# Order tables of the two-level product passes and the closing tiles of a Hymba decode step

## The reference, cut to what matters

```python
def layer(h, pos, conv_prev, ret_prev, norm_mix, w_in, conv_w, w_out,
          norm_mlp, w_up, w_down, ret_fn):
    hn = rmsnorm(h, norm_mix)
    z = hn @ w_in
    u_in, c_gate, b_gate, q, k, v, g = jnp.split(z, SPLITS, axis=-1)
    conv_y, conv_state = causal_conv3(conv_prev, c_gate * u_in, conv_w)
    y_conv = b_gate * conv_y
    ...
    o, ret_state = ret_fn(q, k, v, ret_prev.astype(q.dtype))
    y_ret = head_rmsnorm(o).reshape(Bsz, T, RET_WIDTH) * jax.nn.silu(g)
    h = h + jnp.concatenate([y_conv, y_ret], axis=-1) @ w_out
    hn2 = rmsnorm(h, norm_mlp)
    h = h + jnp.square(jax.nn.relu(hn2 @ w_up)) @ w_down
    return h, conv_state, ret_state
...
    y_prompt = rmsnorm(hp, norm_final)[:, N_META:]
    y_sample = rmsnorm(hs, norm_final)
```

## Time and profile before

| | us |
|---|---|
| median of 3 runs | 1171.07 (1168.94 to 1172.07) |
| the profiled execution | 1170.56 |
| its span, first to last instruction | 1168.8 |
| TensorE busy | 1145.3 (98%) |
| VectorE busy | 764.9 (65%) |
| GpSimd busy | 551.0 (47%) |
| ScalarE busy | 434.7 (37%) |
| mean granted TensorE clock | 0.996 |

### The profile page before, as it was taken

How to read it: one execution, slowest core, us unless ns; L and a number is a source line. 1 busy time by engine, 2 the same in 40 slices (tenths; PEclk the granted TensorE clock), 3 DMA queues, 4 the chain that set the end, 5 groups by cost and what they waited for, 6 DMA issues and landing times.

```text
span 1168.8 us, 22531 instructions
## 1 busy us (share of the span) xinstructions
PE 1145.3 (98%) x8689; PEld 1119.8 (96%) x8689; DVE 764.9 (65%) x1141; ACT 434.7 (37%) x853; POOL 551.0 (47%) x541
## 2 busy tenths in 40 slices
PE   9999999999999999989999999999999999999996
PEld 7899999999999999989999999999898999999996
DVE  4355446456355676787777776777866677777756
ACT  6423313214124433533333333335434444444413
POOL 0154242253150431044232322323989998888992
PEclk9999999999999999999999999999999999999999
DMA  6431211211201222254435353437854553454213
GB/s 202 132 110 36 79 50 54 74 54 54 74 19 57 80 89 87 74 163 134 166 118 181 109 166 130 138 120 257 277 186 129 177 169 103 146 176 136 89 38 146
DMA packets 154007, 139.79 MB, mean 120 GB/s; under 512 B 6809, under 2 KB 118146, under 8 KB 153916
## 3 DMA queue, kind: packets, MB, share of 16 engines
q1 hardware_dynamic: 148814, 135.50, 36.3%
q10 hardware_dynamic: 5102, 3.05, 0.9%
HBM read 98.07 MB, written 40.47 MB: 119 GB/s over the span
## 4 chain that ended last, share of the span: by engine, by line
PE 46%; POOL 3%; DVE 3%; DMA 1%; issue 1%; ACT 0%; SPq 0%; ACTq 0%; POOLq 0%; DVEq 0%
PE pair L1819 15%; PE pair L1820 15%; PE pair L1821 15%; POOL dn_lo L755 2%; DMA m_raw<-m_dram 1%; DVE m_lo L1440 1%; DVE y_out L1557 1%; PE pair L1870 0%; DVE hid L1585 0%; POOL dn_s L743 0%; DVE hid L1459 0%; POOL dn_s L745 0%; ACT m_hi L1058 0%; POOL dn_s L748 0%; POOL dn_s L746 0%
## 5 line engine op out<-in xcount | busy, mean ns | idle before, releaser
L1819 PE MATMUL pair<-m_hi,dn_hi 128*128 128x258 f32 x896 | 256.5, 286 | 8.3 <-DVE a L1591 2.8
L1819 PE MATMUL pair<-b_hi,up_hi 128*128 128x258 f32 x896 | 255.0, 285 | 3.2 <-DVE hid L1497 2.2
L1820 PE MATMUL pair<-m_lo,dn_hi 128*128 128x258 f32 x896 | 254.3, 284 | 0.0
L1821 PE MATMUL pair<-m_hi,dn_lo 128*128 128x258 f32 x896 | 254.1, 284 | 0.0
L1820 PE MATMUL pair<-b_lo,up_hi 128*128 128x258 f32 x896 | 253.6, 283 | 0.0
L1821 PE MATMUL pair<-b_hi,up_lo 128*128 128x258 f32 x896 | 252.2, 282 | 0.0
L1620 PE MATMUL pair<-x_hi,w_both 128*128 128x344 f32 (+2 forms) x576 | 188.7, 328 | 0.0
L1622 PE MATMUL pair<-x_hi,w_both 128*128 128x344 f32 (+2 forms) x576 | 184.3, 320 | 0.0
L1621 PE MATMUL pair<-x_lo,w_both 128*128 128x344 f32 (+2 forms) x576 | 184.2, 320 | 0.0
L1819 PEld LDWEIGHTS pair<-m_hi,dn_hi 128*128 128x128 f32 x896 | 169.7, 189 | 11.1 <-POOL dn_lo L755 7.9
L1591 DVE TENSOR_TENSOR hid<-pair,hid 128x516 f32<-128x516 f32 (+1 forms) x194 | 124.5, 643 | 78.9 <-PE pair L1821 77.6
(11 more groups left out here) (205 smaller groups left out, 2141.4 us busy)
## 6 DMA issues: line engine op xcount, KB each, us to landing
m_raw<-m_dram SPq DMA_DIRECT2D x56, 516.0 KB, 5.0
m_dram<-hid SPq DMA_DIRECT2D x64, 258.0 KB, 2.3
up_raw<-w_up_dram SPq DMA_DIRECT2D x32, 512.0 KB, 5.0
dn_raw<-w_down_dram SPq DMA_DIRECT2D x128, 128.0 KB, 2.4
w_raw<-w_in_dram SPq DMA_DIRECT2D x28, 512.0 KB, 3.7
m_dram<-hid SPq DMA_DIRECT2D x16, 774.0 KB, 3.8
h_dram<-hid SPq DMA_DIRECT2D x8, 516.0 KB, 3.2
h_in<-h_dram SPq DMA_DIRECT2D x16, 258.0 KB, 4.3
```

The source lines that it names most:

```text
L1819: m_.matmul(to, shs[k], mhs[k], start=STARTS[i] and k == 0, stop=False, skip_group_check=more)
L1820: m_.matmul(to, shs[k], mls[k], start=False, stop=False, skip_group_check=more)
L1821: ins = m_.matmul(to, sls[k], mhs[k], start=False, stop=k == last, skip_group_check=more)
```

## The change

Four tables of places are rewritten, one copy changes engine, and the closing tiles are cut anew.

1. Up stage, units 0 to 2: `SPLITS` and `LOWS` place the weight parts otherwise; the four `mid_sum` of unit 0 stand behind the read of product 1 and 2 of unit 1, not ahead of them; `scaled(1, .)` stands ahead of `up_low`; some `squared` move by one product.
2. Down stage: `mid_step` gives way to `MID_HIGH` and `MID_LOW`, tables of steps, one pair for block 0 and one for the later blocks; `AHEAD` covers all passes from 5 to 31 by a new formula.
3. Block 0: product 0 is copied from PSUM to `a1` by ScalarE, not VectorE (new semaphore `a1_copied`, for which VectorE and TensorE's product 2 wait).
4. End: the column halves of the last block are 260 and 256; the closing tiles are 0 to 3 as before, then 4 (8 rows, made beside the products), and four late tiles of 128 rows. Six of eight transposes of tile 5 and a first part of its sum of squares stand ahead of the last two products. The norms of tiles 0 to 4 are each written as two halves of 512 values with a read of a product between them.

```diff
-FINAL_AT = {(NW, 3): 0, (NW + 1, 0): 1, (NW + 1, 5): 2, (NW + 2, 3): 3}
-NORM_AT = {(NW + 1, 1): 0, (NW + 1, 3): 1, (NW + 2, 1): 2, (NW + 2, 6): 3}
+FINAL_AT = {(NW, 3): 0, (NW, 6): 1, (NW + 1, 3): 2, (NW + 1, 6): 3, (NW + 2, 2): 4}
+NORM_AT = {(NW, 6): (0, 0), (NW + 1, 0): (0, 1), (NW + 1, 2): (1, 0), (NW + 1, 3): (1, 1), (NW + 1, 6): (2, 0), (NW + 2, 0): (2, 1),
+           (NW + 2, 2): (3, 0), (NW + 2, 3): (3, 1), (NW + 2, 5): (4, 0), (NW + 2, 6): (4, 1)}
+EARLY_AT = (NW + 2, 4)
...
-def mid_step(n):
-
-    return {0: {4: 0}, 1: {1: 1, 4: 2}, 2: {1: 3, 4: 4}, 3: {1: 5, 4: 6}}[n]
+MID_HIGH = ({11: 0, 13: 1, 15: 2, 17: 3, 20: 4, 22: 5, 24: 6}, {4: 0, 6: 1, 8: 2, 12: 3, 15: 4, 19: 5, 22: 6})
+MID_LOW = ({12: 0, 15: 1, 17: 2, 19: 3, 22: 4, 24: 5, 26: 6}, {6: 0, 9: 1, 12: 2, 16: 3, 19: 4, 23: 5, 26: 6})
...
-for _wi in range(5, 10):
+for _wi in range(5, NW):
     for _i in range(7):
-        AHEAD.setdefault(min(28 + (28 * (_wi - 5) + 4 * _i) // 5 + 1, 55), []).append((_wi, _i))
+        AHEAD.setdefault(max(30 + 62 * (_wi - 5) // 10 + 55 * _i // 100, 7 * (_wi - 2) + _i), []).append((_wi, _i))
...
-FINAL = [(l, c, c + P) for l in range(2) for c in (0, P)] + [(0, 256, 384), (None, 496, HALF), (0, 384, 496), (1, 256, 384), (1, 384, 496)]
-REST = 5
+EDGE = (0, 2 * P + 4, HALF)
+FINAL = [(l, c, c + P) for l in range(2) for c in (0, P)] + [(None, 2 * P, EDGE[1]), (0, EDGE[1], 388), (1, EDGE[1], 388), (1, 388, HALF), (0, 388, HALF)]
+REST, FIRST_LATE = 4, 5
+EARLY_F, LATE_F = (0, 1, 2, 4, 5, 6), (3, 7)
...
                     else:
-                        if i:
-                            mid_split(i - 1)
+                        for j in ((), (0,), (1,), (2,), (3,), (4, 5), (6,))[i]:
+                            mid_split(j)
                         down_split(0, i)
...
+                    if b == 0 and i == 0:
+                        act.wait_ge(dn_done, 7 * q + 1)
+                        s.activation(a1[:, n, :].rearrange("p (t c) -> p t c", c=TQ), pair[BANK[0]][:, :, 0:TQ], ACT.Copy).then_inc(a1_copied, 1)
...
                     if i == 0 and b == 0:
-                        d.tensor_copy(to, src).then_inc(dn_read, 1)
+                        dve.wait_ge(a1_copied, q + 1)
+                        if q:
+                            dve.wait_ge(dn_read, 7 * q)
+                        dve.sem_inc(dn_read, 1)
...
-                    elif i < 4:
-                        pe.wait_ge(dn_read, 7 * q + i - 1)
+                    elif i == 2 and b == 0:
+                        pe.wait_ge(a1_copied, q + 1)
...
+                    if (q, i) == EARLY_AT:
+                        final_transposes(FIRST_LATE, EARLY_F, True)
+            final_transposes(FIRST_LATE, LATE_F)
+            for i in range(FIRST_LATE + 1, len(FINAL)):
                 final_transposes(i)
```

More of the change, by code:

```diff
@@ L605, in _ @@
                 sp.wait_ge(f_ready, i + 1)
-                y = y_out[i % 4]
-                if l is not None:
-                    r0 = HALF * l + c0
[L609 to L615, removed]
+                y, n = y_out[i % 4], c1 - c0
+                if l is None:
+                    for half in range(2):
+                        r0 = HALF * half + c0
+                        sp.dma_start(io["y_prompt"][0, r0:r0 + n, :], y[n * half:n * half + n, :]).then_inc(y_stored[i % 4], 16)
+                elif l and c1 == HALF:
+                    sp.dma_start(io["y_prompt"][0, HALF + c0:SEQ, :], y[0:n - SAMPLES, :]).then_inc(y_stored[i % 4], 16)
+                    sp.dma_start(io["y_sample"].rearrange("b s d -> (b s) d"), y[n - SAMPLES:n, :]).then_inc(y_stored[i % 4], 16)
+                else:
+                    r0 = HALF * l + c0
+                    sp.dma_start(io["y_prompt"][0, r0:r0 + n, :], y[0:n, :]).then_inc(y_stored[i % 4], 16)
+            for i, count in enumerate((4, 2, 2, 3)):
                 sp.wait_ge(y_stored[i], 16 * count)
@@ L1518, in _ @@
                         up_low(0, 5)
-                    if q == 1 and i < 3:
-                        for j in ((0, 1), (2,), (3,))[i]:
-                            mid_sum(0, j)
+                    if q == 1 and i >= 4:
+                        scaled(q, i - 3)
                     if q < LASTU:
@@ L1524, in _ @@
                             up_low(u, j)
-                    elif i >= 2:
+                    if q == 1 and i in (1, 2):
+                        mid_sum(0, 2 * i - 2)
+                        mid_sum(0, 2 * i - 1)
+                    if q == LASTU and i >= 2:
                         mid_low(i - 2, 0)
@@ L1599, in _ @@
                     if b < BLOCKS - 1:
[L1600 to L1602 removed]
+                        for half in range(2):
+                            if 7 * n + i - half in MID_LOW[b > 0]:
+                                mid_low(7 * (b + 1) + MID_LOW[b > 0][7 * n + i - half], half)
                     if (q, i) in NORM_AT:
[L1604 to L1606 removed]
+                        final_norm(*NORM_AT[(q, i)])
+            first_sums()
+            for i in range(FIRST_LATE, len(FINAL)):
                 final_norm(i)
@@ L1854, in _, with final_transposes @@
                         row_sums(i)
-            def final_transposes(i):
+            def final_transposes(i, fs=range(KT), early=False):
                 l, c0, c1 = FINAL[i]
-                pe.wait_ge(closed, 12 if i < 4 else 21)
-                if i == 4:
+                if early:
+                    pe.wait_ge(closed, 18)
+                    pe.wait_ge(dn_read, 7 * (ND - 1))
+                else:
+                    pe.wait_ge(closed, 12 if i < FIRST_LATE else 21)
+                if i == FIRST_LATE and not early:
                     pe.wait_ge(dn_read, 7 * ND)
+                    pe.wait_ge(fsq_done, FIRST_LATE + 1)
                 if i in (2, 3, 4, 5):
@@ L1867, in final_transposes @@
                     pe.wait_ge(gathered, 16)
-                for f in range(KT):
+                for f in fs:
                     src = rest_f[:, f, :] if l is None else acc(f % 4, 2 * (f // 4) + l)[:, c0:c1]
```

128 lines of the change are left out of this document (73 added, 55 removed).

## The result

| | before | after |
|---|---|---|
| median of 4 runs each | 1171.57 us | 1164.30 us |
| their range | 1168.94 to 1173.13 | 1163.58 to 1164.48 |
| profiled run | 1170.56 | 1164.33 |
| its span | 1168.8 | 1162.5 |
| ratio, with its 95% interval | | 0.9939 (0.992 to 0.9958) |

The change is faster, by 7.3 us where 14.9 were predicted, and 1164.3 lies above the top of the range, 1163.5. Half of the gain came.

A forecast was written before the change was run, and what follows sets the result against it. TensorE, 98% busy, bounds the kernel, so only its waits (11.1 us in 11 from VectorE), the clock and the end can give. 3.65 + 4.1 + 6.4 + 0.7 = 14.9 us off 1170.56, plus 0.5 for the median: 1156.2 us, range 1152.8 to 1163.5.

The forecast's parts named there:

- Part 1: Up stage: earlier VectorE reads of products 1 and 3 in unit 1 remove two TensorE waits; 3.65 us, bounds 0 to 3.65.
- the nine instructions: Up stage, unit 1: VectorE's weight parts, sums and scaling behind product 1's read, some 0.62 us each from 511.0.
- the sum stays: VectorE-GpSimd exclusion, weighed for block 1: the forecast's total gain, 14.9 us, was left unchanged.
- Part 2: Down stage, block 0: six waits go, but the one for ScalarE's copy grows to about 1.1 us; gain 4.1, bounds 2.5 to 5.2.
- Part 3: Down stage, block 1: earlier high parts remove the longest wait, two shorter ones and the clock's fall; 6.4 us, bounds 1.2 to 6.4.
- part 4: Later blocks: high parts come up to three products earlier, no wait removed or added; cost 0, bounds 0 and 9 us.
- The lead of GpSimd: Down stage: GpSimd's low parts ahead of TensorE by 3.5 us at pass 6, some 7 us by pass 11.
- The rival on GpSimd: Down stage: GpSimd becomes the bound, seven passes each losing about 1.2 us, 8.5 in all: 1164.7 us; chance 0.07.
- The first rival: Block 1: the long wait stays, the high part still behind GpSimd's sums, clock falls; price 4.9 us, 1161; chance 0.15.
- The slower rival: Blocks 2 to 7: ScalarE waits for loads, delaying GpSimd and TensorE; 4 us in each of six blocks, 1180 us; chance 0.06.
- Part 5: The end: 14 more transposes inside the loop, four late scalings instead of five; gain 0.7 us, bounds -1.0 and 2.0.
- hiccups: The end: reads that now fall beside transposes lose less, taking the sum from -0.55 to about -0.8 us.

The follow-up runs named there:

- Experiment 1: Changed kernel with the up stage of before (its tables, squares and combinations): 1164.91 us, ratio 0.9942.
- 2: Changed kernel with GpSimd's four sums for units 2 and 3 cut from 512 to 32 columns (output differs): 1158.86 us, ratio 0.99.
- 3: Changed kernel with unit 1's four combinations moved in unit 2 behind the reads of products 1 and 2, all work done: 1160.86 us, ratio 0.9912.
- Experiment 6: Changed kernel with unit 1's combinations later, plus pass 0's stored hidden values loaded ahead of the up stage's last two stores: 1159.84 us, ratio 0.9908.
- 7: Changed kernel with unit 1's combinations later, plus GpSimd making half of each weight low part in passes 1-4 and 6-16 (output differs): 1157.77 us.
- 9: Changed kernel with unit 1's combinations later, plus activation loads first in blocks 1 and 3 alone and pass 14's high parts reordered on ScalarE: 1159.13 us.
- 4: Changed kernel with the closing tiles of before (columns, order of transposes and scalings, GpSimd's gathering, halves of 258 columns): 1164.84 us, ratio 0.9939.
- Experiment 8: Changed kernel with unit 1's combinations later, plus early transposes one product later and the eight-row tile's scalings behind the last read: 1158.8 us.
- 12: Kernel before with the down stage's part of the change alone; up stage and closing tiles as before: 1163.57 us, ratio 0.994.
- 11: Changed kernel with units 2 and 3's weight low parts as plain VectorE copies, one SBUF input instead of two (output differs): 1161.09 us, ratio 0.9921.
- 10: Changed kernel with all repairs: later combinations, earlier hidden loads, reordered end, activation loads first in blocks 1 and 3, block 0's product 6 high part later: 1155.7 us.
- experiment 5: Changed kernel with unit 1's combinations later, plus activation loads first in all later blocks and pass 14's high parts reordered on ScalarE: 1169.25 us.

## Why the prediction was half right

**Part 1, 3.65 us predicted, -1.2 came. This is the step that failed.** Its account of unit 1 holds: the last of the nine instructions was to be done near 516.7 and is at 516.6 (L1501). But it ended with "the weight part a product later, still some 6 us ahead of its use in unit 2". No queue of VectorE was written down for unit 2, only for the part moved. All that was moved later is done there, beside GpSimd's sums and ahead of the read due near 532. Experiment 1 shows that the part is worth nothing, 2 that the collisions alone make the wait, and 3 that the place of the read does so as well: take away either, and it goes. Without the wait TensorE would have come to product 3 of that unit 4.0 us earlier than before (the last matmul ahead of it starts at 533.08, before at 537.04); VectorE's read came 0.8 earlier (535.53, before at 536.35). With the wait gone the time is 1158.9 us (2) or 1160.9 (3), inside the predicted range.

The prediction weighed the rule of the Trainium skill ("SBUF — State Buffer", SBUF: two separate sides) that VectorE and GpSimd exclude each other, for the down stage only, and said that the sum stays. In the up stage the six longest of these instructions between 519 and 534 cost 1.35 to 1.78 us in place of 0.68, and the wait, with its clock, 4.8.

**Part 2, 4.1 predicted, 3.4 came.** ScalarE, then SyncE:

```profile
816.95 0.58 ACT L1132 ACTIVATE a<-pair 128x516 f32<-128x516 f32 x1
```

```profile
813.07 3.08 SPq L533 DMA_DIRECT2D m_dram<-hid  x2
816.44 1.76 SPq L573 DMA_DIRECT2D h_in<-h_dram  x4
```

The copy stands on ScalarE where the text has it and ends at 817.5, predicted 817.6. That the two agree is luck: the forecast counts in a trace whose pass 0 begins at 813.45, and here it begins at 814.20. From that start the copy is done after 3.3 us, not 4.15, and the wait for it is 0.4 us, not 1.1. The other wait, 0.92 us, is the one that was overlooked. Before, one of 0.93 us stood there behind two low parts on VectorE, and the forecast let it go; now the read waits for the load of the stored hidden values, which SyncE issues behind two stores. Part 2 followed VectorE and ScalarE and not that queue. Experiment 6 shows it.

**Part 3, 6.4 predicted, 5.2 came; part 4, 0 predicted, 1.5 lost.** The mechanism holds: the long wait went with its clock (0.78 in the earlier trace rows), and no pass of blocks 4 to 7 waits until the closing tiles. The lead of GpSimd, 3.5 us by pass 6, was worked out with TensorE earlier and GpSimd's own times as before, and with 9.1 us of work a pass. Its passes follow each other more slowly than that: the low parts of pass 4 end at 860.7 before and 860.4 now, those of pass 12 at 938.9 and 939.1, 9.8 us a pass in both, while TensorE begins pass 12 at 939.0 and not 946.7. In block 0 GpSimd is already busy 94% of the time (39.8 of 42.3 us). At pass 6, by the prediction's own measure, the lead is 1.0 us (877.1 to 878.1). So GpSimd does not come earlier, and so the loads and high parts that stand behind it are late by 1.0 and 1.3 us. Experiments 7 and 9 show it from both sides: with GpSimd's work less, or with the loads (and in block 3 the high part) ahead of what waits for it, the waits go. The rival on GpSimd had this mechanism at 8.5 us; here it cost 2.7. The first rival, priced at 4.9 us, shows in block 3 and not in block 1: a high part behind weight parts that wait 5.64 us for GpSimd, at 1.5 us here, and at 3.7 with the fallen clock in the traces of experiments 1 and 4. The slower rival did not happen: all loads together kept ScalarE's high parts waiting 18.3 us where it was 13.1:

```profile
L1072 ACT ACTIVATE m_hi<-m_raw 128x1032 fp32r<-128x1032 f32 x56 | 59.0, 1055 | 18.6 <-DMA m_raw<-m_dram 18.3
```

**Part 5, 0.7 predicted, 0.4 came up to the last scaling.** A wait of 0.5 before the early transposes was foreseen and is 0.56. The late transposes wait 1.02 us where 0.57 stood in the earlier trace rows, which is the 0.5 foreseen for half a scaling ahead of the last read. The last product comes 1.7 us later (predicted 1.6), and the first late scaling 2.65 us behind it (2.75). Missed are the 0.25 us for "hiccups", of which nothing came, and the late scalings, which start 1.43 us apart in the mean, against 1.385 in the earlier trace rows:

```profile
1148.14 0.84 PE L1923 MATMUL pair<-ident,hid 128*128 128x128 f32 x6 [0.56 <-DVE y_out L1591]
...
1151.42 3.03 PE L1923 MATMUL pair<-ident,hid 128*128 128x128 f32 x26 [1.02 <-DVE hid L1639]
```

```profile
1150.24 0.74 DVE L1591 SCALAR_TENSOR_TENSOR y_out<-pair,small,gain_f 8x512 f32<-8x512 f32 x1
1150.91 0.40 DVE L1639 TENSOR_TENSOR hid<-pair,hid 128x256 f32<-128x256 f32 x1
...
1157.19 1.28 DVE L1586 SCALAR_TENSOR_TENSOR y_out<-pair,small,gain_f 128x1024 f32<-128x1024 f32 x1
```

Experiment 8 shows that the order alone made the first wait and half of the second, worth 1.0 us.

What the 0.4 us is worth at the end of the span is less. From the start of pass 32 to the end it is 34.1 us before and in experiments 4 and 12, which have the old end; with the new end it is 33.9 in the trace of the changed kernel, but 34.3 to 34.5 in experiments 1, 2, 3, 6, 7, 9 and 11. What follows the last scaling, the last store above all, is 0.25 to 0.8 us longer, where the sum added 0.1; why is not shown. In experiments 8 and 10 it is 33.4 and 33.3 us.

The range was too narrow since each part's bounds were those of its own waits, between nothing and all of them gone. A part that moves work has a bound below nothing: what it does to the next unit. Part 5 had one; part 4's, a loss of up to 9 us, was left out of the range.

## What to carry to other kernels

Where an instruction is moved later, write down the whole queue of its engine until the place where it would have stood anyway is passed, unit by unit, with the lengths that instructions have beside their neighbours, not their shortest. A gain on TensorE is kept only if every engine that feeds it comes earlier too: one that is full in the stage before keeps its times, and all that stands behind it, loads of SyncE included, becomes the next wait. A load that waits for one engine and stands ahead of one that feeds another is safe only while the first of them is already past.

## What was not expected of the hardware

- VectorE's copies from fp32 with one input in SBUF exclude GpSimd's sums as instructions with two do: 0.41 us alone, 1.51 and 1.52 beside them. Reads with one input in PSUM keep their 0.69 us beside GpSimd's sums (at 519.01 and 526.01 in the changed kernel's trace). The Trainium skill ("SBUF — State Buffer", Who interferes with whom) has this: a copy or cast may enter a mode that uses both ports, and then contends. The trace agrees, and the expectation of experiment 11 had left it out.
- The granted clock fell to the lower of its two levels behind single waits of 3.0 us (0.54 over 536.5 to 540 in the changed kernel), of 2.66 and 2.55 us (0.52 over 990.5 to 994, 0.51 over 1034.8 to 1038.3 in experiment 5), and of 1.75 and 1.73 us (0.87 over 952 to 965 in experiment 1 and over 953 to 966 in experiment 4). It stayed at 1.00 behind waits of 1.27 to 1.34 us, but also behind one of 1.79 (experiment 5, 1079 to 1083) and of 2.22 (experiment 1, 520 to 560): the wait's length alone doesn't tell whether it falls.
